# Two expert-choice expert layers: outputs summed in the residual buffer, gate projections in the first group, seven first-group weight slots outside the ring

## The reference, cut to what matters

```python
def expert_choice_moe(x, router_w, w1, w3, w2):      # 16 experts, cap = 32 tokens each
    aff = softmax(x @ router_w)
    gates, idx = lax.top_k(aff.transpose(0, 2, 1), cap)
    xg = x[idx]                                       # (16, 32, 1024)
    hid = silu(xg @ w1) * (xg @ w3)                   # w1, w3: 1024 x 1024 per expert
    ye = (hid @ w2) * gates                           # w2: 1024 x 1024 per expert
    return zeros.at[idx].add(ye)
...
ffn = expert_choice_moe(x, router_w[i], w1[i], w3[i], w2[i])
ple = sigmoid(x @ ple_gate_w[i] + ple_gate_b[i]) * (p[i] @ ple_w[i])
x = layer_norm(DEEPNORM_ALPHA * x + ffn + ple, ln2_g[i], ln2_b[i])
```

## Time and profile before

| | |
|---|---|
| Median of 3 runs | 2349.44 us (2345.97 to 2351.41) |
| The profiled execution's own time | 2344.03 us |
| Its span, first to last instruction | 2342.3 us |
| Mean granted TensorE clock | 0.886 |
| PE busy / DVE busy / ACT busy | 78% / 18% / 17% |
| DMA | 715.95 MB, mean 306 GB/s |
| Chain that ended last | PE 57%, DMA 30%, DVE 6%, ACT 2% |

### The profile page before, as it was taken

How to read it: one execution, slowest core, us unless ns; L and a number is a source line. 1 busy time by engine, 2 the same in 40 slices (tenths; PEclk the granted TensorE clock), 3 DMA queues, 4 the chain that set the end, 5 groups by cost and what they waited for, 6 DMA issues and landing times.

```text
span 2342.3 us, 31246 instructions
## 1 busy us (share of the span) xinstructions
PE 1817.8 (78%) x13163; PEld 1143.8 (49%) x13163; DVE 429.5 (18%) x958; ACT 403.4 (17%) x829; POOL 0.6 (0%) x5
## 2 busy tenths in 40 slices
PE   5989889989898989899966666656789657576565
PEld 4857655557676655586723223212567323232122
DVE  2232311112523101124300001000253101010001
ACT  3031211122523111124200001000233101010001
POOL 0000000000000000000000000000000000000000
PEclk8999799999898999999988879787899788888787
DMA  9768399975554999832299999999822699999993
GB/s 358 228 235 316 152 400 397 388 224 198 214 201 163 369 395 395 281 122 72 72 370 414 420 414 418 422 421 422 267 73 72 260 418 417 421 412 421 422 422 143
DMA packets 181017, 715.95 MB, mean 306 GB/s; under 512 B 27373, under 2 KB 94873, under 8 KB 108569
## 3 DMA queue, kind: packets, MB, share of 16 engines
q1 hardware_dynamic: 180172, 712.29, 77.6%
q10 hardware_dynamic: 716, 1.81, 0.2%
HBM read 826.25 MB, written 1.05 MB: 353 GB/s over the span
## 4 chain that ended last, share of the span: by engine, by line
PE 57%; DMA 30%; DVE 6%; ACT 2%; SPq 2%; issue 2%; ACTq 0%; POOLq 0%; DVEq 0%
DMA ring<-in_w 23%; PE ps L874 19%; PE ps L1182 6%; PE ps L1271 6%; DMA ring<-in_moe_w_up 6%; PE ps L1294 3%; PE ps L1168 3%; PE ps L1192 2%; PE ps L1209 2%; PE ps L857 2%; PE ps L975 2%; PE ps L1153 2%; PE ps L939 1%; SPq L810 1%; PE ps L1111 1%
## 5 line engine op out<-in xcount | busy, mean ns | idle before, releaser
L1271 PE MATMUL ps<-ring,ptb 128*32 128x512 f32 x2048 | 309.5, 762 | 219.4 <-DMA ring<-in_w 211.9
L1271 PEld LDWEIGHTS ps<-ring,ptb 128*32 128x32 f32 x2048 | 85.3, 135 | 438.2 <-issue 435.9
L1294 PE MATMUL ps<-ring,kT 128*32 128x512 f32 x1024 | 151.5, 747 | 86.7 <-DMA ring<-in_w 86.7
L874 PE MATMUL ps<-xT,ring 128*128 128x256 f32 (+2 forms) x640 | 149.7, 395 | 17.1 <-DVE yT L2188 9.5
L874 PEld LDWEIGHTS ps<-xT,ring 128*128 128x128 f32 (+2 forms) x640 | 120.7, 191 | 43.2 <-DVE yT L2188 11.1
L1294 PEld LDWEIGHTS ps<-ring,kT 128*32 128x32 f32 x1024 | 40.5, 133 | 190.9 <-issue 190.0
L874 PE MATMUL ps<-oT,ring 128*128 128x256 f32 x512 | 112.8, 380 | 2.7 <-DVE oT L1919 1.6
L874 PE MATMUL ps<-hT,ring 128*128 128x256 f32 x480 | 108.4, 384 | 5.3 <-ACT hT L1557 5.3
L1182 PE MATMUL ps<-ring,yT 128*32 128x256 f32 x1536 | 92.6, 399 | 17.1 <-DMA ring<-in_moe_w_up 16.3
L874 PEld LDWEIGHTS ps<-oT,ring 128*128 128x128 f32 x512 | 97.0, 190 | 16.8 <-DVE oT L1971 2.0
L2182 DVE TENSOR_TENSOR kT<-pb,ps 128x1024 f32<-128x1024 f32 x8 | 9.8, 1222 | 519.0 <-ACT pb L1712 519.0
(11 more groups left out here) (387 smaller groups left out, 1901.1 us busy)
## 6 DMA issues: line engine op xcount, KB each, us to landing
ring<-in_w SPq DMA_DIRECT2D x384, 1024.0 KB
ring<-in_moe_w_gate SPq DMA_DIRECT2D x96, 1024.0 KB
ring<-in_moe_w_up SPq DMA_DIRECT2D x96, 1024.0 KB
ring<-in_moe_w_down SPq DMA_DIRECT2D x96, 1024.0 KB
ring<-in_ada_w SPq DMA_DIRECT2D x48, 1024.0 KB
ring<-in_diff_w_in SPq DMA_DIRECT2D x12, 1024.0 KB
ring<-in_w_o SPq DMA_DIRECT2D x8, 1024.0 KB
ring<-in_ple_gate_w SPq DMA_DIRECT2D x8, 1024.0 KB
```

The source lines that it names most:

```text
L874: last = mmul(o, l, r, start=start, stop=stop)
L1271: last = mmul(ps[32 * j:32 * j + 32, 2 * a + h, 0:width], xg[:, k, 32 * j:32 * j + 32], w[j][:, ff * k2 + width * h:ff * k2 + width * h + ...
L1294: last = mmul(ps[32 * j:32 * j + 32, 6 + h, :], hidT[:, c, 32 * j:32 * j + 32], w[j][:, D * c2 + 512 * h:D * c2 + 512 * h + 512], start=(c ...
```

## The change

It does five things, in both late layers alike.

1. **Seven guests.** Slots 12 to 18 of group 0 no longer go through the ring. They are read straight into SBUF tensors that are not used at that time (yT, cosd, wr, rows1, gw, rtmp, two stretches of the constants, vt, qT, pb, kT, sqb), in 17 DMAs of 256 or 512 KB, each guest with a semaphore of its own. SP issues guests 0 to 2 when att_go has come, 3 and 4 after the last v_done, 5 and 6 after the norm's sq_mm. The ring's numbers skip them (slot2). rows1 and gw get 128 partitions, and one constant moves so that 512 columns in a row are free.
2. **Gates.** All four gate projections stand between the gather and down of group 0, with their four slots at that place of the ring. ScalarE puts their result into vt instead of kT.
3. **Sum in the residual.** yT is no longer the sum. In group 0 the DVE makes hT = gate * value and xT = ALPHA * xT + hT; the group outputs are then added into xT. The memset of yT and second_sum are gone.
4. **The end.** The last group's output goes to the banks in another order (last_bank), each pair of chunks is signalled by itself (y_pair) and added by itself; the extra gather is gone.
5. **Loops.** The groups are written out. The transposed hidden goes to pb instead of the upper half of kT, and the output copy to kT instead of qT.

```diff
@@ -207,6 +209,25 @@
+        hid2, hidT2 = hid, pb[:, :, :].rearrange("p b n -> p (b n)").rearrange("p (c s) -> p c s", s=P)
+        Yg2 = hid2
...
+        const4 = CONST["slots"][0], CONST["cos_m"][0]
+        guests = [[tiles(yT, 0, 4), tiles(yT, 4, 4)],
+                  [tiles(cosd, 0, 2), wrb[:, 0:512], rows1b[:, 0:1024]],
+                  [tiles(gwb, 0, 2), rtmp[:, :]] + [cst[:, at:at + 512] for at in const4],
+                  [vt[:, 0:1024], vt[:, 1024:2048]],
+                  [tiles(qT, 0, 4), tiles(qT, 4, 4)],
+                  [pb[:, :, :].rearrange("p b n -> p (b n)"), tiles(kT, 0, 4)],
+                  [tiles(kT, 4, 4), sqb[:, :]]]
+        GUESTS = tuple(range(12, 12 + len(guests)))
+
-        E2_PARTS = [range(0, 1), range(1, 2), range(2, E2_GROUPS)]
-        GATE_PARTS = [range(0, 2), range(2, 4)]
-        slot_part = {}
+        up_slots, rest_slots = {}, {}
 
         def moe2_slots(layer):
 
             ph[f"value{layer}"] = len(jobs)
             ple_value_jobs(layer)
+            up_slots[layer] = n_slot[0]
+            n_slot[0] += 32 - len(GUESTS)
             ph[f"gate{layer}"] = len(jobs)
-            for part, groups in enumerate(E2_PARTS):
-                slot_part[2 + layer, part] = n_slot[0]
-                n_slot[0] += 48 * len(groups)
-                if part < len(GATE_PARTS):
-                    ple_gate_jobs(layer, GATE_PARTS[part])
-
-        def gate_jobs(layer, part):
-            return [ph[f"gate{layer}"] + a for a in GATE_PARTS[part]]
+            ple_gate_jobs(layer, range(4))
+            rest_slots[layer] = n_slot[0]
+            n_slot[0] += 16 + 48 * (E2_GROUPS - 1)
+
+        def last_bank(pair):
+
+            return (pair + 3) % 4
+
+        def slot2(layer, i, s):
+
+            if i == 0 and s < 32:
+                return up_slots[layer] + s - sum(x < s for x in GUESTS)
+            return rest_slots[layer] + 48 * i + s - 32
 
...
@@ -797,18 +819,45 @@
-            def load_experts2(l, part):
-                n0, groups = slot_part[2 + l, part], E2_PARTS[part]
+            def load_experts2(l):
...
-                with sp.Fori(0, len(groups)) as i:
-                    order = [(w, j, kk) for kk in range(4) for w in (w1, w3) for j in range(4)]
-                    order += [(w2, j, kk) for kk in range(4) for j in range(4)]
-                    for s, (w, j, kk) in enumerate(order):
-                        sp.wait_ge(S("slot_used"), 48 * i + (n0 + s - RING + 1))
-                        sp.dma_start(ring[:, (n0 + s) % RING, :], w[l, 4 * i + (4 * groups[0] + j)][:, SLOT * kk:SLOT * kk + SLOT])\
-                            .then_inc(S(f"slot{(n0 + s) % RING}"), 16)
+                order = [(w, j, kk) for kk in range(4) for w in (w1, w3) for j in range(4)]
+                order += [(w2, j, kk) for kk in range(4) for j in range(4)]
+
+                def rows(i, s):
+                    w, j, kk = order[s]
+                    return w[l, 4 * i + j][:, SLOT * kk:SLOT * kk + SLOT]
+
+                def expert_slots(i, ss):
+                    for s in ss:
+                        n = slot2(l, i, s)
+                        load(n, ring[:, n % RING, :], rows(i, s))
+
+                def load_guests(gs):
+                    for g in gs:
+                        at = 0
+                        for piece in guests[g]:
+                            n = piece.shape[-1]
+                            sp.dma_start(piece, rows(0, GUESTS[g])[:, at:at + n]).then_inc(S(f"guest{g}"), 16)
+                            at += n
+                        assert at == SLOT
+
+                expert_slots(0, range(0, 7))
+                sp.wait_ge(S("att_go"), 3 + l)
+                load_guests(range(0, 3))
+                sp.wait_ge(S("v_done"), st_span[("mla", "gqa")[l]][-1]["n"] + 1)
+                load_guests(range(3, 5))
+                expert_slots(0, range(7, 11))
+                sp.wait_ge(S("sq_mm"), 6 + 2 * l)
+                load_guests(range(5, 7))
+                expert_slots(0, range(11, 12))
+                expert_slots(0, range(12 + len(GUESTS), 32))
+                load_jobs(f"gate{l}")
+                expert_slots(0, range(32, 48))
+                for i in range(1, E2_GROUPS):
+                    expert_slots(i, range(48))
...
-            def experts2(m, part):
+            def experts2(m):
...
+                                if k2 and h and not (i == 0 and s + j in GUESTS):
+                                    last.then_inc(S("slot_used"), 1)
...
-                    pe.wait_ge(S("xg_ready"), i + (x0 + 1))
-                    pe.wait_ge(S("y_added"), i + (g0 + m - 1))
+                    pe.wait_ge(S("xg_ready"), n)
+                    if i:
+                        pe.wait_ge(S("y_added"), n - l - 1)
+                    gate_up(i)
...
-                    pe.wait_ge(S("hidT_ready"), i + (g0 + 1))
-
-                    pe.wait_ge(S("D_ready"), i + (x0 + 2))
-                    gather(range(C)).then_inc(S("xg_mm"), 1)
-                    pe.wait_ge(S("C_ready"), i + (g0 + 1))
+                    pe.wait_ge(S("hidT_ready"), n)
+                    if i + 1 < E2_GROUPS:
+                        pe.wait_ge(S("D_ready"), n + 1)
+                        gather(range(C)).then_inc(S("xg_mm"), 1)
+                    if i == 0:
+                        project(span[f"gate{l}"])
+                    pe.wait_ge(S("C_ready"), n)
+                    down(i)
...
-                            pe.wait_ge(S(f"Y_ready{c // 4}"), i + (g0 + 1))
-                        last = mmul(ps[:, c // 2, T * (c % 2):T * (c % 2) + T], Yg[:, P * c:P * c + P], Cg[:, :],
+                            pe.wait_ge(S(f"Y_ready{c // 4}"), n)
+                        if i == 0 and c == 0:
+                            await_need(pe, ("job", span[f"gate{l}"][-1]))
+                        b = c // 2 if i < E2_GROUPS - 1 else last_bank(c // 2)
+                        last = mmul(ps[:, b, T * (c % 2):T * (c % 2) + T], Yg2[:, P * c:P * c + P], Cg[:, :],
                                     start=True, stop=True)
-                    last.then_inc(S("y_mm"), 1)
+                        if i == E2_GROUPS - 1 and c % 2:
+                            last.then_inc(S("y_pair"), 1)
+                    if i < E2_GROUPS - 1:
+                        last.then_inc(S("y_mm"), 1)
...
@@ -1484,11 +1528,7 @@
-            for part in range(len(E2_PARTS)):
-                experts2(2, part)
-                if part < len(GATE_PARTS):
-                    pe.wait_ge(S("y_added"), moe_g0[2] + E2_PARTS[part][-1] + 2)
-                    project(gate_jobs(0, part))
+            experts2(2)
...
@@ -2080,7 +2111,6 @@
             def route2(m):
-                V.memset(yT[:, :, :], 0.0).then_inc(S("y_added"), 1)
...
-                    dve.wait_ge(S("y_added"), i + (g0 + m - 1))
-                    V.tensor_tensor(yT[:, :, :].rearrange("p c t -> p (c t)"), yT[:, :, :].rearrange("p c t -> p (c t)"),
-                                    psf(0, 4), ALU.add).then_inc(S("y_added"), 1)
-                assert at_link[0] == n_links, at_link[0]
...
-            def embedding(m, part):
-
-                for a in GATE_PARTS[part]:
-                    dve.wait_ge(S("proj_evac"), acts_before[ph[f"gate{m - 2}"] + a] + 1)
-                    link(V.tensor_tensor(pair_dst(kT, a), pair_dst(kT, a), pair_dst(hT, a), ALU.mult))
-                    last = V.tensor_tensor(pair_dst(yT, a), pair_dst(yT, a), pair_dst(kT, a), ALU.add)
+            def embedding(l):
+
+                for a in range(4):
+                    dve.wait_ge(S(evacuated(span[f"gate{l}"][a])[0]), evacuated(span[f"gate{l}"][a])[1])
+                    last = V.tensor_tensor(pair_dst(hT, a), pair_dst(hT, a), vt[:, 512 * a:512 * a + 512], ALU.mult)
                 link(last)
-
-            def second_sum(m):
                 for a in range(4):
-                    V.scalar_tensor_tensor(pair_dst(xT, a), pair_dst(xT, a), ALPHA, pair_dst(yT, a), ALU.mult, ALU.add)\
-                        .then_inc(S("x_summed"), 1)
+                    last = V.scalar_tensor_tensor(pair_dst(xT, a), pair_dst(xT, a), ALPHA, pair_dst(hT, a),
+                                                  ALU.mult, ALU.add)
+                link(last)
+
+            def experts2(m):
+                l = m - 2
+                dispatch2(0)
+                for i in range(E2_GROUPS):
+                    n = E2_GROUPS * l + i + 1
+                    if i + 1 < E2_GROUPS:
+                        dve.wait_ge(S("D_ready"), n)
+                        dve.wait_ge(S("xg_mm"), n)
+                        dve.wait_ge(S("C_mm"), n)
+                        dispatch2(4 * (i + 1))
+                    dve.wait_ge(S("sg_ready"), n)
+                    V.tensor_tensor(hid2, sg[:, :], psf(2, 2), ALU.mult).then_inc(S("hid_ready"), 1)
+                    dve.wait_ge(S("hT_mm"), n)
```

(12 more changed lines are left out.)

199 lines of the change are left out of this document (69 added, 130 removed).

## The result

The changed kernel takes 2324.11 us (median of 4 runs, 2323.29 to 2324.54), the kernel before 2350.43 us (4 runs, 2345.97 to 2353.31). The ratio is 0.989, with a 95% interval of 0.9875 to 0.9905: 26 us, or 1.1%, faster.

What follows compares the result with a forecast made beforehand. The weights' arrival by DMA was taken to bound the expert parts. Per layer 17.4 - 7.3 + 3.1 = 13.2 us, two layers 26.4: 2317.6 us profiled, 2323.0 on the runs' median, range 2307 to 2337.

Steps and rivals of the forecast that it cites:

- Guests, 17.4 us per layer: Expert parts: seven slots fewer through the DMA after the start, 2.485 us each, saving 17.4 us per layer.
- The place and shape of the hole: Group 0: during the four-gate pause the ring fills and the DMA idles; slots 42, 43 and 44 are held back.
- the prediction's list of signs: What the changed kernel's profile should show if right or wrong, including a single 64-record project pass on PE in group 0.
- The hole's size, 7.3 us per layer: Group 0: slot 44 starts at 1264.1 instead of 1256.8, a delay of 7.3 us per layer, bounds 3.8 to 11.
- The end, 3.1 us per layer: Last group's output: adding pairs while PE still spreads the next ones starts the norm's sums sooner, gaining 3.1 us per layer.
- Edits at nothing: Removed memset, residual sum, written-out loops and new waits: hidden under PE, down or waits for weights, costing nothing.
- One sign that the prediction had named as wrong: Stages ahead of the experts: attention or w_o taking longer than now would count against the forecast; no size given.
- No bubble: Rival, group 0's ring: gate slots come free early enough, so no delay; 2308 us, chance 0.12.
- The guests buy little: Rival: the seven slots' time returns as idle DMA, gates taking 1.47 times their time; 2349 us, chance 0.08.
- Slower: Rival, group 0: gates run wholly at PE's lower clock, 14.1 us each, delay 35.5 us; about 2379 us, chance 0.04.

Runs made afterwards that it cites:

- the late issue: The changed kernel with all seven guests issued only after the norm's sums of squares, none during attention: 2325.81 us.
- the second profile: The changed kernel run and profiled once more, unaltered: 2321.58 us.
- the last experiment: The changed kernel and the kernel before, each run and profiled once more, unaltered: 2321.58 us and 2348.39 us.

## Why the prediction was right

It gave 2323.0 us with a range of 2307 to 2337; measured were 2324.11. The profiled pair came to 2323.29 where 2317.6 had been worked out; of that 5.7 us, 5.2 is the loss ahead of the experts, and the choice to put the gain on the median of the runs instead of on the profiled time is what kept the forecast close. The mechanism is the one forecast, but that the gain came out at 26.3 us against 26.4 is in part luck: the hole was put 1.8 us (in the odd layer 1.4) too small, and the end 1.2 us too small, of which 1.0 came from the clock, so that two errors partly cancelled. By steps:

- **Guests, 17.4 us per layer.** Right: 17.2 and 16.9 in the trace and 17.8 by the medians. They lay hidden, and even the late issue left room.
- **The place and shape of the hole.** Right. Gates predicted to begin 55.5 us after the experts' start (1231.2 - 1175.73) began at 55.9; their length was 27.8 instead of 28.2; down's first block ended at 87.2 us instead of 87.4. Three slots were held back, as said. (The single pass has 128 records in the trace, not the 64 of the prediction's list of signs.)
- **The hole's size, 7.3 us per layer.** The step that was mis-sized; it measured 9.1, and 8.7 in the odd layer. Two things were wrong in it. The DMA had filled the ring 74.7 us after the start instead of 76.1. Slot 31's block did begin when it was forecast (40.0 us after the start, forecast 39.8), but its transfer was put 0.7 us ahead of that, while the gate slots' weak rate shows from 1218 on, 3 us ahead of the block. And the delay was counted to the first byte of slot 44: its ramp, 139 and 360 GB/s in two windows, is 0.8 us more. Slot 44's first bytes came some 0.3 us sooner than forecast (88.1 us after the start instead of 88.4). 7.3 + 1.4 + 0.8 - 0.3 = 9.2. The last slot's block was forecast 10 us earlier behind the experts' start and came 8.0 and 8.2 us earlier, for the same reason.
- **The end, 3.1 us per layer.** From the copy of the output to the end of the sums 11.2 us became 7.8 (1646.89 to 1654.72), so 3.4. The other 1.0 of the 4.3 in the account is the last block at 5.35 us instead of 6.31, which is the clock (0.50 for about 3 us of it, and for 5 us in the kernel before) and no work of the change: in the variant with the gates between blocks it took 6.5 again.
- **Edits at nothing.** No cost of theirs shows: the page's whole slices of the expert parts stand at 420 to 422 GB/s but for the one with the hole, and 17.4 less the hole leaves 8.3 and 8.7 us per layer where 8.0 and 8.2 were measured. One sign that the prediction had named as wrong did appear, attention and w_o longer than before (by 1.9 us, and 2.2 in the second profile); the rows of the last experiment put the first of these down to the clock ahead of the guests, and the average over the profiles gives the guests no part in it.
- **The account of the chances.** "No bubble", 2308, is what moving the gates gives: the variant took 2304.75. "The guests buy little", 2349, needed gates of about 10.4 us each, and they took 6.95. "Slower" had the right mechanism and price, and didn't occur, because the granted clock was 1.00 (the level of 2.4 GHz) in the windows of the gates. It came back just in time: behind the wait and the transposes it fell to 0.50 from 1232 to 1235, under the gather, which took 5.47 us, as it did in the kernel before. The Trainium skill's "TensorE: Matmul & The Clock Gate", section "Part 4: PE-mode transpose", holds that transposes don't raise the clock. The trace agrees in so far as the clock fell behind them, but waits of 2.5 and 1.3 us stood beside them and no run tells the two apart; the gates behind the gather ran at the upper level, so the rule put no price on them.
- The Trainium skill's "DMA: Bandwidth & Descriptors", section "Where 436 GB/s comes from", puts the limit between HBM and SBUF at about 358 GB/s per core, though it also notes a measured 425. No run here agrees with the limit: full slices of every page show 421 to 422 GB/s, and the guests' 16.9 to 17.8 us per layer are seven slots at that rate, not the 20.5 worked out from the limit.

## What to carry to other kernels

Where a ring feeds an engine that waits for weights, work that needs few bytes belongs into the waits between blocks, not into one pause: in these runs the pauses that the ring's depth in time (here 29.8 us) covered left no hole, and once the ring was full each further us of pause cost 1 us. Look for the loads that a ring can't take because it is full, not because the DMA is busy, and for buffers that are idle at that moment: each slot of 1 MB loaded early was worth its 2.5 us. When a hole in the transfers is costed, count the ramp behind each separate restart, and put a gain found in one profile on the median of the runs.

## What was not expected of the hardware

At every restart that was looked at, the transfers came back with a weak stretch: 147 and 303 GB/s in the kernel before, 115 and 172, then 139 and 360 GB/s in the change, in windows of 1 us, against 421. A slot let in by itself (1 MB, 2.5 us at full rate) took about 4 us of windows. The untouched stages ahead of the even experts don't repeat as the expert parts do: two profiles of one program differ there by 1.5 to 1.7 us, and all ten by up to 15.7 us, while the expert parts repeat within 0.3 us. The same 64 records took 15.5 to 17.1 us, by how long the granted clock stood at 0.50 in them.
